# A two-layer decoder step on one core: inputs laid out as long runs, two queues at the start, and high parts made on GpSimd

## The reference

```
y  = gelu(x @ w_y + b_y)
u  = x @ w_x + b_x
xc = conv_b + sum(conv_w[k] * upad[:, k:k + T] for k in range(4))      # width-4 causal convolution over tokens
r  = sigmoid(xb @ w_ga + b_ga);  gi = sigmoid(xb @ w_gi + b_gi)        # 8 blocks of 128 x 128
a  = exp(-8 * r * softplus(-lam));  b = sqrt(1 - a*a) * gi * xc
h[t] = a[t] * h[t-1] + b[t]
out = (h * y) @ w_out + b_out
```

## Time and profile before

| what | value |
|---|---|
| median of 3 runs | 1061.94 us (1060.14 to 1062.6) |
| the profiled execution, its own time | 1060.25 us |
| its span in the trace | 1058.5 us |
| PE busy | 1041.5 us, 98% of the span |
| DVE busy | 839.9 us, 79% |
| ACT busy | 661.5 us, 62% |
| POOL busy | 227.6 us, 22% |
| moved by DMA | 139.54 MB, mean 132 GB/s |

### The profile page before, as it was taken

One profiled execution on the slowest core, in us unless ns is written; L12 is line 12 of the kernel. 1 busy time (PEld: TensorE's weight loads), 2 busy tenths in 40 slices (PEclk: granted clock), 3 DMA queues, 4 the chain that ended last, 5 costly groups with the idle time before them and its releaser, 6 DMA issues.

```text
span 1058.5 us, 21606 instructions
## 1 busy us (share of the span) xinstructions
PE 1041.5 (98%) x8247; PEld 1016.3 (96%) x8247; DVE 839.9 (79%) x1283; ACT 661.5 (62%) x1159; POOL 227.6 (22%) x285
## 2 busy tenths in 40 slices
PE   8999999999999999999999999999999999999996
PEld 8999999999999999999999878999999999999995
DVE  6999898979779697696974664888879697696885
ACT  5999858665736647463666775675836647457432
POOL 2111032011111111103334564210111111111023
PEclk9999999999999999999999999999999999999997
DMA  7323214478877877875131221164777877878502
GB/s 256 121 91 100 81 60 143 98 161 163 176 167 156 196 160 154 202 171 189 40 121 47 65 62 37 41 181 79 159 170 158 197 159 153 203 159 177 136 11 75
DMA packets 54460, 139.54 MB, mean 132 GB/s; under 512 B 5632, under 2 KB 21440, under 8 KB 54368
## 3 DMA queue, kind: packets, MB, share of 16 engines
q0 software_dynamic: 14512, 53.60, 29.9%
q1 hardware_dynamic: 39584, 84.32, 24.4%
q10 hardware_dynamic: 288, 0.59, 0.2%
HBM read 135.95 MB, written 3.56 MB: 132 GB/s over the span
## 4 chain that ended last, share of the span: by engine, by line
PE 89%; DVE 3%; ACT 3%; issue 2%; POOL 1%; DMA 1%; SPq 0%; ACTq 0%; DVEq 0%; POOLq 0%
PE bank L2492 8%; PE bank L2218 8%; PE bank L2494 8%; PE bank L2493 8%; PE bank L2219 8%; PE bank L2220 8%; PE bank L2473 7%; PE bank L2475 7%; PE bank L2474 7%; PE bank L2305 3%; PE bank L2307 3%; PE bank L2306 3%; PE bank L2613 1%; PE bank L2587 1%; PE bank L2446 1%
## 5 line engine op out<-in xcount | busy, mean ns | idle before, releaser
L835 ACT ACTIVATE w_hi<-stage 128x1024 fp32r<-128x1024 f32 x164 | 168.3, 1053 | 127.9 <-DMA stage<-w_up 73.4
L1355 DVE TENSOR_TENSOR w_lo<-stage,w_hi 128x1024 fp32r<-128x1024 f32 x164 | 196.9, 1219 | 54.2 <-ACT w_hi L835 54.2
L2492 PE MATMUL bank<-part_hi,w_hi 128*128 128x272 f32 x672 | 195.5, 291 | 0.0
L2494 PE MATMUL bank<-part_hi,w_lo 128*128 128x272 f32 x672 | 193.6, 288 | 0.0
L2493 PE MATMUL bank<-part_lo,w_hi 128*128 128x272 f32 x672 | 193.1, 287 | 0.0
L2218 PE MATMUL bank<-x_hi,w_hi 128*128 128x288 f32 (+1 forms) x496 | 145.3, 293 | 1.7 <-issue 1.0
L2219 PE MATMUL bank<-x_lo,w_hi 128*128 128x288 f32 (+1 forms) x496 | 143.8, 290 | 0.0
L2220 PE MATMUL bank<-x_hi,w_lo 128*128 128x288 f32 (+1 forms) x496 | 143.1, 289 | 0.0
L2492 PEld LDWEIGHTS bank<-part_hi,w_hi 128*128 128x128 f32 x672 | 126.4, 188 | 2.9 <-issue 1.8
L2493 PEld LDWEIGHTS bank<-part_lo,w_hi 128*128 128x128 f32 x672 | 126.5, 188 | 0.0
L2494 PEld LDWEIGHTS bank<-part_hi,w_lo 128*128 128x128 f32 x672 | 126.5, 188 | 0.0
(11 more groups left out here) (292 smaller groups left out, 2910.4 us busy)
## 6 DMA issues: line engine op xcount, KB each, us to landing
stage<-w_up SPq DMA_DIRECT2D x54, 512.0 KB, 3.8
stage<-w_down SPq DMA_DIRECT2D x52, 512.0 KB, 4.3
stage<-w_down POOLq DMA_DIRECT2D x48, 512.0 KB, 5.6
stage<-w_up POOLq DMA_DIRECT2D x44, 512.0 KB, 5.7
stage<-w_qkv SPq DMA_DIRECT2D x10, 512.0 KB, 4.5
stage<-w_x SPq DMA_DIRECT2D x8, 512.0 KB, 5.1
stage<-w_y SPq DMA_DIRECT2D x8, 512.0 KB, 3.4
stage<-w_out SPq DMA_DIRECT2D x8, 512.0 KB, 3.7
```

The source lines that it names most:

```text
L835: A(w_hi[:, slot_of(l, k), :], raw_of(l, c, k), ACT.Copy).then_inc(s_whi, 1)
L1355: vt.tensor_tensor(w_lo[:, s, :], raw_of(l, c, k), w_hi[:, s, :].bitcast(F32), ALU.subtract)\
L2492: mm(out, wh, xh[:, k, :], start=(fresh and k == 0), stop=False, skip_group_check=True)
L2494: ins = mm(out, wl, xh[:, k, :], start=False, stop=(k == 1), skip_group_check=True)
```

## The change

It has five parts.

1. **Layout.** x, w_x, w_y, gate weights, w_out, w_qkv and w_o are put into DRAM slab by slab, so that each partition of a slab is one run of 4 KB. x comes as `x_a` (first 256 tokens) and `x_b` (the others), four pieces each. In SBUF an x piece still is two runs for each partition. The gate weights become one load in place of two.
2. **Start.** ACT issues the four pieces of `x_a` first of all; SP issues slabs 0 and 1 in halves of 512 columns (`load_front`, `load_back`), then slabs 2 and 3, the early part of `vecs`, the four pieces of `x_b`, the gates, and the late part of `vecs`. ACT and DVE split x pieces and slab halves in turn, and PE's first products wait for halves. y(0) is done feature tile by feature tile, each with a wait for its own slab, and so is x(1), with a wait for its own piece of x. `WARM` is 9.
3. **High parts on POOL.** The high parts of the four x/y slabs of pairs 1, 2 and 3 (12 slabs, `POOL_HI`) are made by POOL (`slab_hi`); ACT's `split` leaves them out.
4. **Order on DVE in step 0.** The convolution comes first; the split of the second half of x and the small operations on `lam` (`derive_in`, `derive_series`) come behind it. ACT's exp for them moves too.
5. **`residual0`** is no longer paced by the convolutions: it runs in groups of 8, 4 and 4 between the calls of `slab_hi`.

The diff, cut to its core:

```diff
-WARM = 13
+WARM = 9
...
+        POOL_HI = [job_at[("pair", p)][0] + k for p in range(1, 4) for k in range(4)]
...
+            late = VEC["sinks"][0]
+            for j in range(2):
+                load_front(j)
+                load_back(j)
+            load_slabs(("pair", 0), w_in, 2, 2, 2)
+            sp.dma_start(vecs[:, 0:late], vec[:, 0:late]).then_inc(s_vec, 16)
             for p in range(4):
                 if p == 0:
-                    sp.dma_start(acc[:, :, 256:512],
-                                 xp_t[:, 256:512].rearrange("(k p) t -> p k t", p=128)).then_inc(s_xb, 16)
-                    sp.dma_start(acc[:, :, 512:TOK], xs_t.rearrange("(k p) t -> p k t", p=128)).then_inc(s_xb, 16)
+                    for k in range(4):
+                        load_x_rest(k)
...
 # ACT
+                    if j in POOL_HI:
+                        continue
...
+            for k in range(4):
+                act.dma_start(acc[:, 2 * k:2 * k + 2, 0:256], x_a[k].rearrange("p (k t) -> p k t", k=2))\
+                    .then_inc(s_xa[k], 16)
+            for j in range(2):
+                x_split(0, [2 * j])
+                front(j)
+                x_split(0, [2 * j + 1])
+                back(j)
...
 # DVE
-            derive_in()
-            derive_series()
             for s in range(8):
...
                 if s == 0:
+                    x_split(1)
                     conv_lo(0)
                     split([4])
+                    derive_in()
+                    derive_series()
                     derive()
...
 # POOL
+            def slab_hi(p):
+
+                for k in range(4):
+                    j = job_at[("pair", p)][0] + k
+                    hi, _, raw = split_targets(j)
+                    pool.wait_ge(s_arrived[where[j][0]], where[j][1])
+                    if jobs[j][1] >= SLOTS:
+                        pool.wait_ge(*free_at[jobs[j][1] - SLOTS])
+                    pt.tensor_copy(hi, raw).then_inc(s_whip, 1)
+
+            slab_hi(1)
+            residual0(0)
+            slab_hi(2)
+            residual0(1, range(4))
+            slab_hi(3)
+            residual0(1, range(4, 8))
...
 # PE
+                    group_by_k(range(2), 0, pair_pieces(w0),
+                               lambda k: ((s_xlo, k // 2 + 1), (s_wlo if k % 4 > 1 else s_frontlo, k // 4 + 1)))
+                    group_by_k(range(mark[("y", 0)], mark[("y", 0)] + 2), 0, pair_pieces(w0 + 2),
+                               lambda k: ((s_wlo, j + 3 + k // 4),))
```

More of the change, by code:

```diff
@@ L108, with build @@
 SUM_ORDER = (S1, S3, S2, S4)
-def build(nc, xp_t, xs_t, vec, w_y, w_x, w_ga, w_gi, w_out, w_qkv, w_o, w_up, w_down,
+def build(nc, x_a, x_b, vec, w_in, w_gates, w_out, w_qkv, w_o, w_up, w_down,
           ck_t, cache_k, cache_v, y_t, small, k_p, v_p, k_s, v_s):
@@ L676, in load, with load_slabs @@
                 put(where[j][0], src)
[L678 to L684, removed]
+            def load_slabs(name, w, first, n, jj=0):
+                for k in range(n):
+                    load(job_at[name][0] + jj + k, w[first + k])
             def bring(l, c, k, on, src, after):
@@ L760, in _ @@
[L760 to L765, removed]
+                    for k in range(4):
+                        load_x_rest(k)
+                else:
+                    load_slabs(("pair", p), w_in, 4 * p, 4)
@@ L766, in _ @@
+                load(job_at[("gates", p)][0], w_gates[p])
+                if p == 0:
+                    sp.dma_start(vecs[:, late:NVEC], vec[:, late:NVEC]).then_inc(s_veclate, 16)
             for g in range(2):
-                load_quad(("o", 0, g), ov, g)
+                load_slabs(("o", 0, g), w_out, 4 * g, 4)
             load_mlp(0)
             for g in range(2):
-                load_quad(("qkv", g), qv, g)
-            load_pair(("qkv", 2), qv, 1024)
-            load_quad(("o", 1, 0), pv, 0)
+                load_slabs(("qkv", g), w_qkv, 4 * g, 4)
@@ L774, in _ @@
+            load_slabs(("qkv", 2), w_qkv, 8, 2)
+            load_slabs(("o", 1, 0), w_o, 0, 4)
             sp.wait_ge(s_tokc, 3)
@@ L780, in _ @@
                       .then_inc(s_kv_kept, 16)
-            load_quad(("o", 1, 1), pv, 1)
+            load_slabs(("o", 1, 1), w_o, 4, 4)
             load_mlp(1)
@@ L962, in _ @@
                     break
+                if s == 0:
+                    act.wait_ge(s_sp, 1)
+                    A(tiny[:, 2, :], tiny[:, 1, :], ACT.Exp, scale=-1.0).then_inc(s_spe, 1)
                 if s >= 2:
@@ L1415, in _, with front, back @@
             vt.memset(tiny[:, 7, :], 0.0).then_inc(s_hlo, 2)
[L1416 to L1420, removed]
+            def front(j):
+                hi, lo, raw = split_targets(j)
+                dve.wait_ge(s_fronthi, j + 1)
+                vt.tensor_tensor(lo[:, 0:512], raw[:, 0:512], hi[:, 0:512].bitcast(F32), ALU.subtract)\
+                    .then_inc(s_frontlo, 1)
+            def back(j):
+                hi, lo, raw = split_targets(j)
+                dve.wait_ge(s_whi, j + 1)
+                vt.tensor_tensor(lo[:, 512:1024], raw[:, 512:1024], hi[:, 512:1024].bitcast(F32), ALU.subtract)\
+                    .then_inc(s_wlo, 1)
+            for j in range(2):
+                x_split(0, [2 * j])
+                front(j)
+                x_split(0, [2 * j + 1])
+                back(j)
             split([2, 3])
@@ L1537, in _ @@
                 c0, n = HALF[h]
[L1538 to L1540 removed]
+                if s:
                     split(next_jobs(s)[:1])
```

113 lines of the change are left out of this document (53 added, 60 removed).

## The result

The changed kernel takes 1071.79 us (median of 5 runs, 1070.29 to 1072.1), the kernel before 1061.94 us (5 runs beside it, 1060.14 to 1062.6): ratio 1.0094, 95% interval 1.0083 to 1.0104. It is slower by 9.9 us; the forecast was 1070.0 and slower. The profiled execution took 1071.79 us, with a span of 1069.9 us.

A forecast was written before the change was run, and what follows sets the result against it. PE was taken as the bound, with DVE's list from 15 to 127 us a second path as long; -1.4 + 10.8 + 2.0 - 3.1, less 0.15 of slack, made +8.1 us: 1070.0 us, range 1058.9 to 1075.

The forecast's parts named there:

- The two paths: Between 15 and 127 us, DVE's list is as long as PE's; PE gains no more than DVE plus 0.15 us.
- The copies: POOL's 12 copies of 1024 columns each take 0.9 us from DVE: +10.8 us (ends 2.6 and 26).
- 3.1 for waits: DVE's own waits in steps 0, 2 and 4 (0.3, 1.3, 1.1) and ACT's 0.4 take up 3.1 us.
- the scaled scaling operation: Price of one POOL copy to DVE, scaled by columns from a 288-column scaling operation: 0.8 us; 0.9 was taken.
- The rival of the copies that slip in: Copies fit beside DVE's waits and one-input operations at under 0.1 us each: 1059.6 us, or 1058.9; chance 0.24.
- ACT's relief: ACT loses 12 copies of 1.07 us; worth 0.4 us, once, in step 2.
- `residual0`, forecast +2.0: Its 16 operations cost DVE about 0.2 us each, less 1.2 us already showing: +2.0 us on DVE's path.
- The start: Slab 3 and the end of its low part come 1.4 us sooner, near 13.9 us (ends 0.6 and 1.8).
- I take both: At the start, 0.6 us from later vecs bytes and 0.8 us from long runs at 390 GB/s are both counted.
- long runs don't do what they say: Rival: the start gives 0.6 in place of 1.4 us, forecast 1070.8; within the forecast's case, no chance of its own.
- The sum: DVE's path in total: +8.3 us, less PE's slack of 0.15, makes the kernel 8.1 us slower.
- What would show it: Copies of 1.2 us or more, DVE stretched about 0.9, new PE waits of 8 to 10 us, x(1) at 18 to 19.

The follow-up runs named there:

- the run with derivations in DVE's waits: four mends, plus second half of x split before the convolution, early vecs columns by ScalarE, derive_in and derive_series between the first slab's low parts: 1061.29 us.
- the last run: four mends with derive_in moved early, derive_series behind slab 1's low part, x's second half split sooner, residual0 two at a time: 1060.4 us beside 1061.37.
- the first run: Changed kernel with the 12 high parts of pairs 1 to 3 given back to ACT, all else as changed: 1063.82 us.
- the idle copies: Changed kernel with high parts on ACT, and POOL making 12 copies of 1024 columns that nobody uses: 1071.72 us.
- four mends: Changed kernel with high parts on ACT, residual0 paced, x on SyncE's queue and the first halo's memset early: 1061.23 us beside 1061.13 for the kernel before.

## Why the prediction was right

**The two paths.** Right, and the table's last two columns bear it out: fourteen kernels, with output products from 125.98 to 137.35 us, all within 0.03 us of the rule. The 1.9 is the chain from z over `m_hi` and `m_lo` to PE, so it holds wherever PE waits; that PE waits there, in eleven of the fourteen, however early x(1) began, is what the traces show. (The 105.6 was read from the run with derivations in DVE's waits, and stood in the expectation of the last run; those two are the ones in which PE decides. The 1.9 holds in the other twelve.) For the kernel before the two ends lie 0.1 us apart (126.73 and 126.85), so a gain had to come on both; only the last run did that.

**The copies, forecast +10.8 gross, less 3.1 for waits, +7.7 net.** Measured 7.35 net at z(6) (changed kernel against the first run); gross 10.0 us (DVE busy 114.37 against 104.37 us), 0.83 a copy where 0.9 was taken, and 2.65 taken up where 3.1 was. The mechanism was the one in the earlier trace rows. The Trainium skill, "SBUF — State Buffer", section "SBUF: two separate sides", says that GpSimd and a DVE operation with two SBUF inputs, or in a mode that uses both ports, take the shared port pair as an exclusive lock for a whole instruction; the trace agrees that it is the whole instruction, 1.05 us for an operation of 8 columns beside a copy of 1.04. Of the four prices weighed, the scaled scaling operation (0.8) was nearest; the copy's own time was estimated at 1.4 us and is 1.14. The rival of the copies that slip in fails on the rows above: none ran free.

**ACT's relief, forecast 0.4.** None shows, by the idle copies.

**`residual0`, forecast +2.0.** Right in sign: 1.22 at z(6), 1.03 in time.

**The start, forecast -1.4.** This step failed: +1.95 us at z(6) and +1.9 in time (interval 0.5 to 2.7), with high parts on ACT and paced `residual0` against the kernel before. Two things were wrong. "I take both" counted bytes and a mean rate up to slab 3, and left out by which queue the pieces come: from 3 to 12.3 us, when the last x piece was taken up, ACT's queue moved 1.03 MB and SyncE's 2.33 MB, and x was what was waited for, not slab 3 (moving x: 1.23 us). And the price of the new order left out whom the first halo waits behind (1.06 us). The rate was wrong too: 390 GB/s were taken, and from 3 to 9 us the changed kernel moved 340. With x on SyncE's queue slab 3's low part still ended at 15.2 to 16.1 us in five kernels, and not at 13.9: neither the 0.8 us of the long runs nor the 0.6 of the bytes of `vecs` shows, which is worse than the rival "long runs don't do what they say" had it. The rest of the new start (slab halves, y(0) tile by tile, nine warm-up products) was not tried by itself.

**The sum.** At z(6) 7.35 + 1.22 + 1.95 = 10.52 us, which is 135.47 - 124.95, as these are steps from one to the other. The forecast had 7.7 + 2.0 - 1.4 - 0.15 = 8.1. In time 9.9 us stand against 8.1: the range held it, by the size of its bounds for the copies and not by its bounds for the start (0.6 to 1.8 us sooner), which were both on the wrong side. The start missed by 3.35 us; the copies (0.35) and `residual0` (0.8) missed the other way and hid a third of that, which was luck.

**What would show it.** Copies at 1.14 us, a little under the 1.2 named; DVE operations stretched by 0.85 for 0.9; new waits of PE before the gates of steps 3 and 5 and for `m_lo`, as named, but in all 6.5 us with the one before x(1), since that one took the part of step 1. x(1) came at 24.56 in place of 18 to 19, and with no harm: DVE decided.

## What to carry to other kernels

Before work is moved to GpSimd, look not at how idle it is but at what VectorE does at that time: a copy in SBUF there cost VectorE some 0.8 ns a column here, whoever used the result, and what VectorE's own waits absorbed was a fixed amount (2.65 us, with whole copies as with half ones). Where two engines' lists are equally long, read both ends (here x(1) + 105.6 and z(6) + 1.9) before an edit, and price an edit on the later one. When a start is rearranged, follow each small thing that another engine waits for, a memset of six columns or a piece on the less served queue, to the place it now has in its engine's list.

## What was unexpected of the hardware

PE's granted clock fell in the changed kernel behind the 2.9 us wait before x(1): 0.52, the lower of the two levels (1.2 GHz), from 24.5 to 31 us, while the run with idle copies waited 3.1 us at the same place and kept 1.00. First the changed kernel, then that run:

```profile
24.50:31.00 6.50, 6.44 (x28) 6.45 (x29) 5.97 (x25) 2.33 (x4) 0.00 (x0) 0.52 0.25 80
```
```profile
24.50:31.00 6.50, 6.34 (x47) 6.34 (x48) 6.01 (x24) 2.83 (x5) 0.00 (x0) 1.00 0.24 80
```

The gates of step 0 begin at 33.78 us in the one and at 31.14 in the other, 2.64 us apart, and z(0) ends at 50.00 and 49.97. So it cost PE 2.6 us and the kernel nothing, as DVE's path hid it. The forecast had taken the clock as unhurt by waits of 1.3 us; why it fell in one of these two and not in the other stays open. In two other runs it was below 1.00 early on, 0.64 (long runs alone) and 0.72 (derivations in DVE's waits) from 9 to 13 us, where the other kernels have 1.00.

The two queues were not served alike: with x on ScalarE's queue its last piece could be split at 12.21 us, on SyncE's, between the slab halves, at 9.66, though ScalarE had issued all four by 3.4 us. And of four kernels with long runs (long runs alone, changed, x on SyncE's queue, four mends) none moved the stretch from 3 to 9 us much faster than the short runs did (346, 340, 283 and 273 GB/s against 342), while from 9 to 13 us they moved 397 to 410 against 367.
